# Prompt attention with the probabilities as fp32r weights and the values streaming three key blocks behind the scores

## The reference, cut to what matters

```python
s_s = einsum('bqhgd,bqhmd->bqhgm', q, k_s) * scale            # selected keys
o_s = einsum('bqhgm,bqhmd->bqhgd', masked_softmax(s_s, m_s), v_s)
s_w = einsum('bqhgd,bwhd->bqhgw', q, kv_w[:, :, 0]) * scale   # window of 512
o_w = einsum('bqhgw,bwhd->bqhgd', masked_softmax(s_w, m_w), kv_w[:, :, 1])
# o_c: the same over the compressed keys
return g[..., 0:1] * o_c + g[..., 1:2] * o_s + g[..., 2:3] * o_w
```

## Time and profile before

| what | value |
|---|---|
| median of 3 runs | 1863.62 us (1863.18 to 1865.58) |
| span of the profiled execution, first to last instruction | 1862.2 us |
| time of the profiled execution outside its span | not recorded; the median is 1.4 us above the span |
| TensorE busy | 1730.0 us, 93% of the span |
| VectorE, ScalarE, GpSimd busy | 942.1, 564.6, 351.0 us |
| attend stage | about 382 to 817 us |

### The profile page before, as it was taken

The page is one execution under the profiler, slowest core; times in us unless marked ns, Lnnn a source line. Parts: engine busy times, 40 slices in busy tenths (PEclk is TensorE's granted clock), DMA queues, the critical chain, the costliest instruction groups (busy, mean ns, idle before and its releaser), DMA issues. The chain is left out here.

```text
span 1862.2 us, 27167 instructions
## 1 busy us (share of the span) xinstructions
PE 1730.0 (93%) x10863; PEld 1490.2 (80%) x10864; DVE 942.1 (51%) x1593; ACT 564.6 (30%) x876; POOL 351.0 (19%) x288
## 2 busy tenths in 40 slices
PE   5999999969989998878979899999999999999988
PEld 4655788956555554547979899999999999999978
DVE  3356216776553444119231455655565566556544
ACT  4001115645443444211132332222232222222232
POOL 0000100042213121212125022222222222222210
PEclk8999999979999999797989899999999999999988
DMA  6312516412326134354040111211112112111102
GB/s 241 70 63 77 222 32 227 176 57 62 102 64 214 57 93 179 119 168 148 4 128 1 42 34 40 62 34 59 42 34 68 34 34 68 34 46 55 34 12 97
DMA packets 90684, 155.15 MB, mean 83 GB/s; under 512 B 15302, under 2 KB 68078, under 8 KB 88254
## 3 DMA queue, kind: packets, MB, share of 16 engines
q1 hardware_dynamic: 76736, 93.13, 15.6%
q0 software_dynamic: 13056, 59.77, 9.8%
q10 hardware_dynamic: 816, 1.18, 0.2%
HBM read 133.61 MB, written 24.83 MB: 85 GB/s over the span
## 5 line engine op out<-in xcount | busy, mean ns | idle before, releaser
L2455 PE MATMUL ps<-h_up,w_split 128*128 128x344 f32 x2112 | 399.5, 321 | 7.1 <-DVE h_rest L2617 5.2
L2627 DVE TENSOR_TENSOR xT<-ps,xT 128x688 f32<-128x688 f32 x352 | 228.2, 690 | 283.3 <-PE ps L2455 268.3
L2455 PEld LDWEIGHTS ps<-h_up,w_split 128*128 128x128 f32 x2112 | 345.0, 189 | 8.9 <-DVE h_rest L2617 4.2
L2455 PE MATMUL ps<-gated,wd_split 128*128 128x344 f32 x1584 | 258.3, 321 | 0.9 <-ACT last_row L2569 0.9
L2455 PEld LDWEIGHTS ps<-gated,wd_split 128*128 128x128 f32 x1584 | 251.0, 188 | 1.6 <-issue 1.1
L2455 PE MATMUL ps<-h_rest,w_split 128*128 128x344 f32 x1056 | 224.8, 321 | 0.4 <-ACT wd_split L2565 0.4
L2455 PEld LDWEIGHTS ps<-h_rest,w_split 128*128 128x128 f32 x1056 | 179.1, 189 | 0.7 <-ACT wd_split L2565 0.7
L2581 POOL TENSOR_TENSOR w_split<-w_raw,w_split 128x1024 fp32r<-128x1024 f32 x44 | 114.3, 2598 | 152.4 <-ACT w_split L2527 152.4
L2541 ACT ACTIVATE hu<-ps 128x1032 f32<-128x1032 f32 x44 | 45.4, 1033 | 314.5 <-PE ps L2455 314.5
L2635 DVE SCALAR_TENSOR_TENSOR cv<-hu,ccol,cv 128x1024 f32<-128x1024 f32 x88 | 129.5, 1472 | 16.4 <-ACT cv L2543 10.7
L1719 DVE TENSOR_REDUCE top<-ps 128x1 f32<-128x384 f32 (+4 forms) x124 | 71.1, 585 | 108.1 <-PE ps L1302 63.2
(11 more groups left out here) (459 smaller groups left out, 2576.4 us busy)
## 6 DMA issues: line engine op xcount, KB each, us to landing
w_raw<-in_w_up SPq DMA_DIRECT2D x44, 512.0 KB, 6.2
wd_raw<-in_w_down SPq DMA_DIRECT2D x22, 512.0 KB, 3.6
unit<-in_cache_kv_win POOLq DMA_DIRECT2D x16, 512.0 KB, 4.5
x_kept<-xT SPq DMA_DIRECT2D x1, 4128.0 KB, 25.2
xT<-x_kept SPq DMA_DIRECT2D x1, 4128.0 KB
xtok<-in_x_prompt SPq DMA_DIRECT2D x2, 2048.0 KB, 8.2
w_qu<-in_w_in SPq DMA_DIRECT2D x2, 2048.0 KB, 8.7
w_out_sb<-in_w_out SPq DMA_DIRECT2D x4, 1024.0 KB, 11.1
```

The source lines that it names most:

```text
L2455: mm = pe.matmul(k.ps[:, bank + c, 0:TG], w(wn), x(xn)[:, c * TG:c * TG + TG], start=start and m == 0, stop=stop and m == 2)
L2627: dve.tensor_tensor(x[:, part], k.ps[:, bank + part.start:bank + part.stop, 0:TG], x[:, part], ALU.add).then_inc(added, 1)
```

## The change

The value product is turned round. The probabilities become the weight (128 keys x 128 queries of one head) and the values move, so that the result has the queries on partitions at once and needs no transpose.

- ScalarE takes the exponential of each score block twice, as fp32 (`raw`) and as fp32r (`high`). GpSimd subtracts `high` from `raw` into `low`, in place. Six such slots (`RING`) replace the buffers of whole branches.
- `v1` and `vc1` hold 130 columns for each block and head: v high, a column of ones, a column of zeros, v rest. GpSimd makes `v1` in the compress stage behind its gather of j = 2 (`split_values`); the copies at the start of the attend stage are gone.
- For each key block and head TensorE loads `high` and moves 130 columns, then loads `low` and moves the first 66. One "value" step does two heads (a `pair`) of one block; pair 0 goes to bank 6 and pair 1 to bank 7. It follows three scores behind the score of its block (`LAG`), pair 1 four behind.
- The copies to `oT` and the transposes are gone. For each branch and pair VectorE takes a reciprocal and adds the two parts by a `tensor_reduce` out of PSUM into `part`, then signals `freed`, on which the first value of the next branch in that bank waits. After pair 1 it multiplies by the gate, scales `part` (now from SBUF) and adds it to `oacc`.
- The list has the turn of group g + 1 ahead of the last score of group g, not behind it. In the planned cost a value step (one pair of one block) counts 0.25 and an out nothing.
- `k_up` moves to other memory, and a wait on `k2_rows` and `k_rest` moves from ScalarE's window exponential to its first "key keep".

The diff, cut to its core (left out: semaphore lists, the old order, the operands of the other lines that are removed):

```diff
 NH2 = NB // 2
+VW = 2 * HD + 2
+VS = VW + 2
+V_BYTES = NT * 2 * NKV * VW * 4
+RING = 6
...
+        def split_values(pool):
+
+            rows = [k.kv[:, 0:NT, KVW * (1 + br) + P:KVW * (2 + br)].rearrange("p t (h d) -> p t h d", h=NKV) for br in range(2)]
+            flat = k.v1[:].rearrange("p t b h d -> p (t b h) d")
+            pool.memset(flat[:, :, HD + 1:HD + 2].bitcast(F32), 0.0)
+            pool.memset(flat[:, :, HD:HD + 1].bitcast(F32), 1.0)
+            for br in range(2):
+                pool.tensor_copy(k.v1[:, :, br, :, 0:HD], rows[br]).then_inc(v_upper, 1)
+            for br in range(2):
+                pool.wait_ge(v_upper, br + 1)
+                pool.tensor_tensor(k.v1[:, :, br, :, HD + 2:VW], rows[br], k.v1[:, :, br, :, 0:HD].bitcast(F32), ALU.subtract
+                                   ).then_inc(k.v_split, 1)
+
...
+                if j == 2:
+                    split_values(pool)
...
+    k.high, k.low, k.raw = [], [], []
+    for n in range(RING - 1):
+        if n == 2:
+            assert o == k.off_v
+            o = k.off_v + V_BYTES
+        high, o = at(f"high{n}", [P, GQA, P], F32R, o)
+        low, o = at(f"low{n}", [P, GQA, P], F32R, o)
+        raw, _ = at(f"raw{n}", [P, GQA, P], F32, o - GQA * P * 4)
+        k.high.append(high)
+        k.low.append(low)
...
+    LAG = 3
...
+    def values_at(n):
+
+        out = []
+        for pair, m in ((1, n - LAG - 1), (0, n - LAG)):
+            if 0 <= m < len(SCORES):
+                out.append(("value", SCORES[m][0], m, pair))
+                if first_last(m)[1]:
+                    out.append(("out", SCORES[m][0], SCORES[m][1], pair))
+        return out
+
     ORDER = [("split", 0), ("split", 1)] + [("look", 0, *s) for s in looks_of(0)] + [("merge", 0), ("turn", 0)]
     for g, (i, kvh) in enumerate(GROUPS):
...
+        mine = [n for n, s in enumerate(SCORES) if s[0] == g]
+        n_looks, n_scores, looks = len(nxt), len(mine) - 1, 0
+        for m, n in enumerate(mine):
+            if m == n_scores and nxt:
+                ORDER += [("merge", g + 1), ("turn", g + 1)]
+            ORDER.append(("score", g, n))
+            while m < n_scores and looks * n_scores < n_looks * (m + 1):
+                ORDER.append(nxt[looks])
+                looks += 1
+            ORDER += values_at(n)
         if g + 2 < len(GROUPS):
...
+        return {"score": 0.45, "look": 0.3, "turn": 0.1, "out": 0.0, "split": 0.0, "merge": 0.0, "value": 0.25}[kind]
     total = sum(cost(step) for step in ORDER)
...
                 elif kind == "value":
-                    br, = rest
-                    bl = blocks_of(i)[br]
-                    pe.wait_ge(powered, scores_to(g, br))
-                    if values:
-
-                        pe.wait_ge(kept, values)
-                    else:
-                        pe.wait_ge(v_set, 2)
-                        pe.wait_ge(v_kept, 2)
-                    for b in bl:
-                        v = k.vc1[:, kvh, :] if br == CMP else k.v1[:, b, br, kvh, :]
-                        mm = pe.matmul(k.ps[0:HD + 1, 6, :], v, probs[br][:, b - bl[0]].rearrange("p h q -> p (h q)"),
-                                       start=(b == bl[0]), stop=(b == bl[-1]))
+                    n, pair = rest
+                    _, br, b = SCORES[n]
+                    first, last = first_last(n)
+                    pe.wait_ge(lowered, n + 1)
+                    if n == 0:
+                        pe.wait_ge(k.v_split, 2)
+                        pe.wait_ge(vc_upper, 2)
+                        pe.wait_ge(v_kept, 1)
+                    if first and (g or br):
+
+                        pe.wait_ge(freed, OUTS.index((g, br, pair)) - 1)
+                    v = k.vc1[:, kvh] if br == CMP else k.v1[:, b, br, kvh]
+                    for h in range(2):
+                        out = k.ps[:, 6 + pair, h * VS:h * VS + VW]
+                        pe.matmul(out, k.high[n % RING][:, 2 * pair + h, :], v, start=first and h == 0, stop=False)
+                        mm = pe.matmul(out[:, 0:HD + 2], k.low[n % RING][:, 2 * pair + h, :], v[:, 0:HD + 2], start=False, stop=last and h == 1)
...
+                    n, = rest
+                    act.wait_ge(scored, n + 1)
+                    if n >= RING:
+
+                        act.wait_ge(valued, VALUES.index((n - RING, 1)) + 1)
+                    if n == RING - 1:
+
+                        act.wait_ge(v_turned, 1)
+                        act.wait_ge(kc_split, 3)
+                    for out in (k.raw[n % RING][:], k.high[n % RING][:]):
+                        act.activation(out.rearrange("p h q -> p (h q)"), k.ps[:, 4 + n % 2, :], ACT.Exp,
+                                       scale=SCALE).then_inc(powered, 1)
...
+                    pool.wait_ge(powered, 2 * n + 2)
+                    pool.tensor_tensor(k.low[n % RING][:], k.raw[n % RING][:], k.high[n % RING][:].bitcast(F32), ALU.subtract
+                                       ).then_inc(lowered, 1)
 
...
+                dve.wait_ge(vc_upper, 1)
+                dve.wait_ge(v_kept, 1)
+                dve.tensor_tensor(k.vc1[:, :, HD + 2:VW], k.ps[:, 6, 0:P].rearrange("p (h d) -> p h d", h=NKV),
+                                  k.vc1[:, :, 0:HD].bitcast(F32), ALU.subtract).then_inc(vc_upper, 1)
...
-                    dve.wait_ge(added, steps + 4)
+                    br, pair = rest
+                    last = max(n for n, s in enumerate(SCORES) if s[:2] == (g, br))
+                    dve.wait_ge(valued, VALUES.index((last, pair)) + 1)
+                    o = k.ps[:, 6 + pair, 0:2 * VS].rearrange("p (h z d) -> p h d z", h=2, z=2)
+                    mine = slice(2 * pair, 2 * pair + 2)
+                    dve.reciprocal(k.norm[:, 0, mine], o[:, :, HD, 0]).then_inc(added, 1)
+                    dve.tensor_reduce(k.part[:, mine], o[:, :, 0:HD, :], AX.X, ALU.add).then_inc(added, 1)
                     outs += 1
+                    dve.wait_ge(added, 2 * outs)
+                    dve.sem_inc(freed, 1)
+                    if pair:
+
+                        z = (1, 2, 0)[br]
+                        gate = k.gates[:, i, 3 * GQA * kvh:3 * GQA * (kvh + 1)].rearrange("p (h z) -> p h z", z=3)[:, :, z]
+                        link(dve.tensor_tensor(k.norm[:, 1], k.norm[:, 0], gate, ALU.mult))
+                        acc = k.oacc[:, i, GQA * HD * kvh:GQA * HD * (kvh + 1)].rearrange("p (h d) -> p h d", h=GQA)
+                        link(dve.tensor_tensor(acc if br == SEL else k.part[:], k.part[:], bc(k.norm[:, 1], 2, HD), ALU.mult))
+                        if br != SEL:
+                            link(dve.tensor_tensor(acc, k.part[:], acc, ALU.add))
```

More of the change, by code:

```diff
@@ L1077, in stage_attend @@
     valued = nc.alloc_semaphore("a_valued")
-    kept = nc.alloc_semaphore("a_kept")
-    turned = nc.alloc_semaphore("a_turned")
-    weighed = nc.alloc_semaphore("a_weighed")
+    lowered = nc.alloc_semaphore("a_lowered")
+    freed = nc.alloc_semaphore("a_freed")
     added = nc.alloc_semaphore("a_added")
@@ L1150, in stage_attend @@
         if g + 2 < len(GROUPS):
             ORDER.append(("split", g + 2))
-        ORDER.append(("value", g, SEL))
-    END = len(GROUPS) - 1
-    ORDER += [("out", END, SEL), ("value", END, CMP), ("out", END, CMP), ("value", END, WINDOW), ("out", END, WINDOW)]
-    SCORES = [step[1:] for step in ORDER if step[0] == "score"]
-    VALUES = [step[1:] for step in ORDER if step[0] == "value"]
-    assert VALUES == [step[1:] for step in ORDER if step[0] == "out"]
+    for n in range(len(SCORES), len(SCORES) + LAG + 1):
+        ORDER += values_at(n)
@@ L1158, in stage_attend @@
+    VALUES = [step[2:] for step in ORDER if step[0] == "value"]
+    OUTS = [step[1:] for step in ORDER if step[0] == "out"]
     LOOKS = [step for step in ORDER if step[0] in ("look", "merge", "turn")]
@@ L1185, in cost @@
         kind, g, *rest = step
-        return {"score": 0.45, "look": 0.3, "turn": 0.1, "out": 0.45, "split": 0.0, "merge": 0.0,
-                "value": 0.86 * len(blocks_of(GROUPS[g][0])[rest[0]]) if kind == "value" else 0.0}[kind]
+        return {"score": 0.45, "look": 0.3, "turn": 0.1, "out": 0.0, "split": 0.0, "merge": 0.0, "value": 0.25}[kind]
     total = sum(cost(step) for step in ORDER)
@@ L1260, in _ @@
             pe.wait_ge(k_rest, 4)
-            looks = scores = values = outs = 0
+            looks = scores = 0
             def to_turn(step):
@@ L1485, in _ @@
             act.activation(k.glog[0:NB, NT], k.glog[0:NB, NT], ACT.Exp, scale=-1.0).then_inc(gated, 1)
-            scores = values = 0
             for step in ORDER:
@@ L1700, in _ @@
             tops_rows(0)
-            dve.memset(k.v1[:].rearrange("p t b h d -> p (t b h) d")[:, :, HD:HD + 1], 1.0).then_inc(v_set, 1)
-            looks = outs = looked_at = 0
+            looks = looked_at = outs = 0
             def weight(row, n):
```

125 lines of the change are left out of this document (33 added, 92 removed).

## The result

The changed kernel takes 1948.61 us (median of four runs, 1939.79 to 1950.12) against 1863.4 us of the kernel before: ratio 1.0443, 95% interval 1.0419 to 1.0468. I forecast 1872.7 us with a range of 1848 to 1894. The direction was right, the time lies outside the range, and the loss is nine times the one that I forecast. One of the six executions of the later run e6_lag4, 2011.86 us, was in a slower state than its others and is left out of that run's median.

The account below looks back on a forecast made before the run. TensorE's own work was taken to bound the attend stage. The terms -1.9 + 4 + 13 - 8 + 2 = +9.1 us on the 1862.2 us span gave 1871.3, and 1.4 us more for the median 1872.7 us, range 1848 to 1894.

Parts of the forecast that it names:

- The granted clock should stay near 1.00 from about 415 us on: Sign to check in the changed profile: TensorE at full clock in the attend stage after its start.
- the start: First groups of the attend stage: half clock may last longer without the dense fp32 values, +2 us, 0 to +10.
- the clock falls: Rival, attend stage: few columns moving beneath long loads put a third at half clock, about 1925 us, chance 0.05.
- VectorE and the holds: Ends of groups: GpSimd's subtractions hold VectorE and its work crowds, +13 us for 16 groups, 0 to +37.
- VectorE bounds the ends of groups: Rival, ends of groups: VectorE's crowding costs 2.3 us a group, 37 us in all, 1897 us, chance 0.08.
- Finer steps, -8 us: Attend stage: values in small pieces spread the sample steps evenly and shorten TensorE's waits, -8 us.
- Values, +12.1: TensorE's value product: 1184 weight loads at 0.117 us replace 296 matmuls, +12.1 us, between -0.9 and +15.7.
- outs, -14: TensorE's 48 outs: their transposes go, -12.0 us, and waits for `oT`, -2 us.
- loads cost less: Rival, value product: a load of probabilities costs 0.0625 us, values 74 us, time 1808 us, chance 0.05.
- ScalarE, +4: Attend stage: 148 more exponentials delay ScalarE's copies for sample steps, mostly covered, +4 us, 0 to 24 for key copies.
- GpSimd, 0: Attend stage: 148 subtractions, 186.8 us, covered by the scores' lag; delayed cache-row fetches cost nothing, bounds 0 and +6.
- Slower: Whole kernel: the outcome of a longer time than before, chance 0.55 in all.

Follow-up runs that it names:

- e6_lag4: The changed kernel with the values four and not three key blocks behind the scores: 1961.48 us, ratio 1.0514.
- e3: The changed kernel without GpSimd's subtraction, ScalarE's exponential written straight into `low` (not the reference's product): 1901.28 us, ratio 1.0211.
- b3: The kernel before, plus a second exponential on ScalarE for each of the 148 scores into a spare buffer: 1871.61 us, ratio 1.0046.
- e4: The changed kernel without GpSimd's subtraction and with 1560 moved columns in a block for 784 (not the reference's product): 1881.29 us, ratio 1.0089.
- b2: The kernel before, plus an unused GpSimd subtraction of 512 columns for each of the 148 scores: 1898.53 us, ratio 1.0184.
- e1: The changed kernel with all 130 columns moved behind `low`, 1040 columns in a block for 784: 1928.97 us, ratio 1.0352.
- e9: The changed kernel with 1560 moved columns in a block for 784 and the subtraction on VectorE instead of GpSimd: 1934.03 us, ratio 1.0363.
- b1: The kernel before, plus a second ScalarE exponential and an unused GpSimd subtraction for each score, through one spare buffer: 1932.49 us, ratio 1.0393.

## Why the prediction was wrong, point by point

- **The step that failed: the clock.** "The granted clock should stay near 1.00 from about 415 us on" was wrong: it stood at half until about 465 us, and again and again behind idle places. I had put +2 us for it in the sum (the start) and 0.05 on the rival "the clock falls". It is +67 of the +74 us of the stage. I had the mechanism in hand, and the price of the rival, 1925 us, was of the right size. I argued it away because scores and looks with full movement lie between the values. At 670 to 710 us they lie there too, and the clock doesn't return. What I lacked is that the question is not only whether the stream drops the clock but how soon it brings it back: idle places were sure to come, there were 42 us of them in the earlier trace rows.
- **VectorE and the holds.** Right in kind, a third too small: 13 us of idling forecast beside bounds of 0 and 37, and about 19 us of idle time went with the subtraction in e3. The idle time of the stage rose by 21 us net. The held time of VectorE is 48 x (442 - 164) + 32 x (520 - 427) + 16 x (628 - 425) + 32 x (528 - 425) ns = 23 us, where I had 37. The rival "VectorE bounds the ends of groups" was half right too: the bank's freeing at line 1777 is TensorE's largest wait. What I left out is that each such idle place also costs the clock, 24 us of the 47 that e3 gave back.
- **Finer steps, -8 us.** Not to be seen net. The waits for units are gone, those for `keyT` fell to 1.3 us, but the sample softmax still costs 9.3 us, and idling as a whole rose.
- **Values, +12.1, and outs, -14.** The pace of 0.117 was a little high, 0.11 at full speed: 1184 x 0.111 = 131.4 us, +5.0 and not +12.1. TensorE's work, counted at full speed, came to -15 us in the stage where I had -1.9; the values explain 7 us of that, the other 6 I can't place. The rival "loads cost less" is refuted by the same rows.
- **ScalarE, +4.** b3 measured +8 us in the old order (interval +5 to +12). What the sum had no term for is TensorE's wait for `q_up`, ScalarE's copies of the queries for the looks: 11.7 us in 10 waits where it was 2.1 us in one. At 652 us the two copies (1.27 us) stand behind the two exponentials of a group's last score and the look stands behind the next score; in the old order the SEL values of a whole branch lay there. It isn't the holds, as it is 11.2 us in e3 and 10.4 in e4, nor the second exponential alone, as it is 2.0 in b3. That the new order did it is argued from the list, no run changed it.
- **GpSimd, 0.** Its own count was right, 189.8 us against 186.8, and TensorE no longer waits for units. But "covered" was said of its queue only; b2 shows that such a load alone (1.04 to 1.08 us a subtraction, less than the 1.29 of the new kernel) costs 34 us through VectorE and the clock.
- **Outside the stage.** From the stage's end to the last instruction the kernel after takes 1054.7 us and the kernel before 1045.4. These 9 us are part of the loss, and the sum had nothing for them. In the runs from e1 to e9 it is 1047.3 to 1053.7, in b1, b2 and b3 1048.6, 1045.6 and 1045.3. Behind the stage's end a wait for a DMA (`hrow`) is longer, 3.1 us against 2.0, a wait for VectorE (`H`, line 2207) too, 5.7 us against 1.1, and half clock lasts some 8 us longer; I made no run on this, and its cause stays open.
- **The chances, and luck.** Slower had 0.55 and came true, for a reason on which I had put 0.05. That the terms besides the clock look right is luck: in the stage they measured +21 - 15 = +6 us where I had +9 - 1.9 = +7, and each of the two is off by 12 or 13 us, in opposite directions.

## What to carry to other kernels

When a product is turned so that its weights change with every few moved columns, price it twice: at the full clock and at half, and ask how soon the stream will have the clock back after the next idle place. Look at the granted clock of the new stream's stretches before its busy share. And before GpSimd gets a steady load beside a VectorE that works in SBUF, list VectorE's instructions with two SBUF inputs and who waits behind them: a subtraction nobody needed cost 1.8% here.

## What the hardware showed that I had not expected

- TensorE stood at 1.2 GHz for some 46 us while busy for nearly all of it; a stretch of the run with twice the moved columns, 80 to 91% busy, stood at 2.4 GHz. Moving columns twice for nothing made the kernel 36.5 us faster.
- A wait of 2.6 us was followed by 46 us of half clock: with its sequel it cost about ten times itself. In the kernel with twice the moved columns a wait of 2.5 us was followed by some 3 us of half clock.
- A VectorE instruction on four elements waited out two GpSimd subtractions in a row (2.78 us from 625.27 us in the kernel after, beside a pair of 2.51 us that ends at 628.01), so that hold wasn't bounded by one instruction of GpSimd.
